# A two-block transformer pass on one Trainium2 core: norm sums in pieces, modulation vectors in the heads, and the state space's discretisation moved to the first output product

## The chip, the cores and the metric

The kernel runs on one core of one Trainium2 chip. The metric is the device time of one execution in microseconds (us); lower is better. In texts and rows PE is TensorE (PEld its weight loads), DVE is VectorE, ACT is ScalarE, POOL is GpSimd, SP is the engine that only issues transfers; a "q" behind a name is the engine's queue of waits, semaphores and DMA issues.

## What is computed

256 tokens of width 2048 go through two blocks, all in float32. Cut to what matters here:

```python
mod = silu(c) @ w_ada + b_ada              # 6 vectors of 2048: shifts, scales, gates
h = rmsnorm(x, g_mix) * (1 + sc1) + sh1
x = x + ga1 * (concat(rmsnorm(attn(h), g_attn), rmsnorm(lru(h), g_lru)) @ w_out)
h = rmsnorm(x, g_ffn) * (1 + sc2) + sh2
x = rmsnorm(x + ga2 * peer(h), g_final)    # peer: top-k experts
# second block, with its own c: s5 state space, then sparse attention
h = modulate(rmsnorm(x, g_l0), ...)
a, bb = s5_discretize(lam, log_step, b)    # exp, sin, cos, a quotient; no token enters
x = x + gate * s5_mixer(h, a, bb, ...)
x = x + gate * nsa_mixer(modulate(rmsnorm(x, g_l1), ...), kv(modulate(rmsnorm(x, g_kv), ...)))
return rmsnorm(x, g_final2)
```

rmsnorm divides by the root of the mean square over the 2048 channels. Channels lie on partitions, in 16 tiles of 128, so x is a buffer of 128 x 16 x 256.

## The kernel before

Each engine has its own hand-written program (`sync`, `tensor`, `scalar`, `vector`, `gpsimd`), and they meet only by semaphores. At a stage's end all four computing engines pass `meet` (L339), which waits for all of them.

**The stream.** All weights come as tiles of 1 MB through a ring of four slots (`load`, L384). SP issues them in one fixed order; a load waits until the slot's user of four loads ago has released it, and every later load waits behind it. `STAGES` (L52) gives each stage's tiles per round. A tile of a product is one 128-column output tile for TensorE (`gemm`, L465); a tile of a modulation matrix is a product with the vector silu(c) that VectorE makes in two halves with a running sum (`whole_vec`, `vec_sum`, L1383 to 1397).

**The first stage** has 8 rounds of four tiles: two for VectorE (the shift vector, `shift_part`) and two for TensorE (the scale vector, rows of one partition, L577). x is the fifth load. ScalarE issues the parameters and 19 transfers for the discretisation (many of them broadcasts of small tables over 16 or 64 partitions), then works on the discretisation between the stage's steps; GpSimd makes its elementwise part (L2021 to 2046) and VectorE the rest, between its tiles (L1474 to 1506). The result is written to memory (L1012) and read back before the recurrence.

**A norm** is a chain over four engines: ScalarE squares x into `SQ` in four calls (`norm_squares`, L954), TensorE multiplies ones with all 16 tiles (`norm_sums`, L548, float32 products run as two passes, so 32 instructions), VectorE takes mean and epsilon for 512 columns (`norm_rstd`, L1417; with one group both halves hold the same), ScalarE the root, VectorE the reciprocal of 512 columns, then 16 multiplications (`norm_scale`), which ScalarE follows with the shift (`norm_bias`). Each chain begins after a `meet`, but for the first, whose sums TensorE makes after its sixth tile. There are seven: mix, merged (two groups: attention and recurrence), ffn, final, l0 (its x is the result of final), l1, final2.

**The heads** are eight rounds of eight tiles: five products and three modulation vectors (positions 2, 5, 7). TensorE's order in a round is three products, the recurrence's gates, half a product, the scores, two halves, the transposes of probabilities, half a product, the attention (L600 to 640). VectorE makes the convolution, the vector of position 2, then waits for the scores and takes the row maxima; ScalarE needs these for the exponentials, VectorE scales the result, and TensorE transposes it.

**The first output product** (`w_out`) has 16 product tiles and 24 modulation tiles, in the order product, vector, product, vector, vector. VectorE adds each product to x when it is done (`residual`) and releases the bank; there are four banks. Its last vectors are shifts and scales of the ffn norm and the last gate. At the start of the next stage GpSimd multiplies the first two vector tiles of that stage (`vec_times`, L2051).

**Final and l0.** After the experts TensorE turns y back tile by tile (L731), VectorE adds it to x (L1789). Then all meet; norm final rewrites x, norm l0 follows in full, then all meet again and the recurrence starts with `fraction` on VectorE and the first product on TensorE.

**The end.** After the last product and a meeting, norm final2; when all 16 tiles are scaled, one transfer of 2 MB writes the result.

## Time and profile before

| what | value |
|---|---|
| runs shown | 3823.6, 3832.76, 3842.07 us (median 3832.76) |
| the profiled execution | 3838.9 us, span of its trace 3837.2 us, granted TensorE clock 0.962 of full |
| busy | PE 94%, PEld 82%, DVE 63%, ACT 35%, POOL 10% |
| instructions | 57514 |
| DMA | 817.73 MB, mean 213 GB/s |

The busy shares of 40 slices of 96 us, in tenths, and the granted clock of TensorE beside them:

```profile
PE   5799987999989999999999997999999899999997
DVE  5443454887547777777777776888816541655664
POOL 3000000420000000000000000677700000000000
PEclk9899999999999999999999998999999996999999
```

A low digit of PE is a stretch in which the engine that carries nearly all the work waits. The first slice is the first stage; the other dips lie at the norms. A clock below 1 in a row is a mean over stretches at the full 2.4 GHz and at 1.2 GHz.

### The profile page before, as it was taken

What the parts mean: (1) busy time and instruction counts of PE and PEld (TensorE: products, weight loads), DVE (VectorE), ACT (ScalarE), POOL (GpSimd) and SP (SyncE); (2) the same over time, 40 slices, a digit from 0 to 9 for tenths busy, and PEclk for the clock granted to TensorE, in tenths of its full rate; (3) what the DMA queues carried; (4) which work ended last, traced back from release to release, by engine and by line L of the source; (5) the groups of instructions that cost most, each with busy time, mean ns of one, the idle gap of its engine ahead of it and who ended that gap; (6) DMA issues with size and microseconds to landing.
All of it is one profiled execution on the core that took longest, in us unless ns stands there. A gap on an engine that the chain in (4) does not pass through costs nothing. (4 is left out here: it accounts for less than half of the span.)

```text
span 3837.2 us, 57514 instructions
## 1 busy us (share of the span) xinstructions
PE 3595.6 (94%) x21190; PEld 3148.6 (82%) x21190; DVE 2425.1 (63%) x4274; ACT 1333.5 (35%) x1967; POOL 390.2 (10%) x402
## 2 busy tenths in 40 slices
PE   5799987999989999999999997999999899999997
PEld 1488876778977999999999995666689899999997
DVE  5443454887547777777777776888816541655664
ACT  1233301212234444444444443211113442555553
POOL 3000000420000000000000000677700000000000
PEclk9899999999999999999999998999999996999999
DMA  8566666655665787887888774222247550555543
GB/s 322 196 226 210 221 241 250 227 203 168 234 258 210 285 297 290 301 300 285 298 288 297 289 290 154 77 87 87 88 154 252 213 179 22 180 182 188 186 170 116
DMA packets 123555, 817.73 MB, mean 213 GB/s; under 512 B 13345, under 2 KB 18721, under 8 KB 27169
## 3 DMA queue, kind: packets, MB, share of 16 engines
q1 hardware_dynamic: 105120, 760.26, 55.0%
q10 hardware_dynamic: 18304, 55.64, 3.8%
q8 instruction: 93, 1.52, 0.2%
q14 instruction: 38, 0.30, 0.0%
HBM read 791.66 MB, written 24.18 MB: 213 GB/s over the span
## 5 line engine op out<-in xcount | busy, mean ns | idle before, releaser
L473 PE MATMUL bank<-H,ring 128*128 128x256 f32 x4352 | 981.5, 384 | 44.8 <-ACT H L969 14.4
L473 PEld LDWEIGHTS bank<-H,ring 128*128 128x128 f32 x4352 | 826.5, 192 | 186.9 <-issue 68.5
L1683 DVE TENSOR_TENSOR vlo<-ring,vhi 128x1024 fp32r<-128x1024 f32 x448 | 548.2, 1225 | 312.1 <-ACT vhi L1141 295.5
L1141 ACT ACTIVATE vhi<-ring 128x1024 fp32r<-128x1024 f32 x448 | 475.0, 1061 | 632.8 <-PE bank L543 350.3
L1402 DVE TENSOR_TENSOR wlo<-ring,whi 128x1024 fp32r<-128x1024 f32 x240 | 293.8, 1225 | 324.0 <-ACT whi L946 317.4
L509 PE MATMUL bank<-Hhi,whi 128*128 128x256 f32 x1920 | 482.0, 288 | 16.4 <-DVE Hlo L1413 9.3
L510 PE MATMUL bank<-Hlo,whi 128*128 128x256 f32 x1920 | 475.3, 285 | 0.0
L536 PE MATMUL bank<-vhi,Ghi 128*128 128x512 f32 x1024 | 400.3, 391 | 0.0
L537 PE MATMUL bank<-vhi,Glo 128*128 128x512 f32 x1024 | 399.9, 391 | 0.0
L509 PEld LDWEIGHTS bank<-Hhi,whi 128*128 128x128 f32 x1920 | 370.0, 193 | 22.0 <-issue 16.2
L488 PE MATMUL bank<-Fhi,vhi 128*128 128x256 f32 x1536 | 374.4, 283 | 0.0
L489 PE MATMUL bank<-Flo,vhi 128*128 128x256 f32 x1536 | 373.6, 280 | 0.0
L510 PEld LDWEIGHTS bank<-Hlo,whi 128*128 128x128 f32 x1920 | 370.6, 193 | 0.0
L946 ACT ACTIVATE whi<-ring 128x1024 fp32r<-128x1024 f32 x240 | 253.9, 1059 | 313.1 <-PE bank L514 292.5
L489 PEld LDWEIGHTS bank<-Flo,vhi 128*128 128x128 f32 x1536 | 288.8, 188 | 0.5
L488 PEld LDWEIGHTS bank<-Fhi,vhi 128*128 128x128 f32 x1536 | 288.5, 188 | 0.5
L543 PE MATMUL bank<-vlo,Ghi 128*128 128x512 f32 x1024 | 276.4, 392 | 12.5 <-DVE vlo L1683 12.5
L1388 DVE CUSTOM_DVE_ANT_0 ring<-ring,cond 128x1024 f32<-128x1024 f32 x192 | 234.5, 1258 | 79.5 <-DMA ring<-in_w_ada 58.8
L514 PE MATMUL bank<-Hhi,wlo 128*128 128x256 f32 x1920 | 270.8, 284 | 0.0
L514 PEld LDWEIGHTS bank<-Hhi,wlo 128*128 128x128 f32 x1920 | 248.9, 192 | 0.0
L543 PEld LDWEIGHTS bank<-vlo,Ghi 128*128 128x128 f32 x1024 | 192.1, 188 | 56.0 <-DVE vlo L1683 15.8
L1760 DVE CUSTOM_DVE_ANT_0 arena<-arena,cond 128x1024 f32<-128x1024 f32 x192 | 233.8, 1218 | 0.0
(384 smaller groups left out, 4401.1 us busy)
## 6 DMA issues: line engine op xcount, KB each, us to landing
ring<-in_peer_u SPq DMA_DIRECT2D x128, 1024.0 KB, 5.0
ring<-in_peer_v SPq DMA_DIRECT2D x128, 1024.0 KB, 4.9
arena<-in_w_mod SPq DMA_DIRECT2D x96, 1024.0 KB, 6.7
ring<-in_w_ada SPq DMA_DIRECT2D x80, 1024.0 KB, 4.9
ring<-in_w_qz SPq DMA_DIRECT2D x64, 1024.0 KB, 4.8
ring<-in_w_in SPq DMA_DIRECT2D x40, 1024.0 KB, 4.8
ring<-in_w_mod SPq DMA_DIRECT2D x32, 1024.0 KB, 5.4
ring<-in_ssm_in SPq DMA_DIRECT2D x32, 1024.0 KB, 4.9
```

The source lines that it names most:

```text
L473: last = mm(out, ring[:, pos % R, k, :], rhs[:, k, :], start=(k == 0), stop=(k == KT - 1))
L488: mm(out, u_hi[:, k, :], Fhi[:, kk, :], start=(kk == 0), stop=False)
L489: mm(out, u_hi[:, k, :], Flo[:, kk, :], start=False, stop=False)
L509: mm(out, whi[:, half, k, :], Hhi[:, kk, :], start=(kk == 0), stop=False)
L510: mm(out, whi[:, half, k, :], Hlo[:, kk, :], start=False, stop=False)
L514: last = mm(out, wlo[:, half, k, :], Hhi[:, kk, :], start=False, stop=(kk == KT - 1))
L536: mm(pair[th][:], G_hi[part][:, n, tok], vhi[:, half, k, :], start=(n == 0), stop=False)
L537: mm(pair[th][:], G_lo[part][:, n, tok], vhi[:, half, k, :], start=False, stop=False)
L543: last = mm(pair[th][:], G_hi[part][:, n, tok], vlo[:, half, k, :], start=False, stop=(n == 7))
L1141: A(vhi[:, half], v_half(pos, half), ACT.Copy).then_inc(s("vhi_ready"), 1)
L1402: v.tensor_tensor(wlo[:, half], ring[:, pos % R, 8 * half:8 * half + 8, :], whi[:, half].bitcast(F32), ALU.subtract).then_inc(s("wlo_ready ...
L1683: v.tensor_tensor(vlo[:, half], v_half(pos, half), vhi[:, half].bitcast(F32), ALU.subtract)\
```

## The change

Four things are done together.

- **First stage.** The discretisation leaves it. Its inputs come as one prepared array in one transfer (`disc_in`), after the merged norm's scaling, and its instructions stand in the first output product: ScalarE's and GpSimd's as one block, VectorE's behind the additions of tiles 5 and 8 to 12. x is loaded after the fourth round, the sums of norm mix come after TensorE's 13th tile. The vector with c in columns is loaded first and passed on at once.
- **Heads.** Each head also loads three modulation vectors beside the ring, into a buffer of their own (`head_vec`), and VectorE multiplies them behind position 2. The first output product's stream is left with its 16 product tiles.
- **Norms in pieces.** ScalarE squares x in pieces of 4, 4, 4, 3 and 1 tiles, each as soon as VectorE has added the tiles (`new_squares` waits for the banks' releases); TensorE makes the sums directly behind the stage's last product, before the meeting. In the heads ScalarE squares each finished tile. Rows and reciprocals take one group only where there is one. Norm final and l0 share one pass: ScalarE also squares x times g_final, both sums are made, l0 is scaled from the unscaled x, and x itself is scaled later, in front of the recurrence.
- **The end.** The result leaves in four transfers, as its tiles are ready.

The diff, cut to its core and without the common indentation of a hunk:

```diff
-STAGES = dict(shift_scale=(4, 8, 4, 2), heads=(8, HEADS, 5, 3), w_out=(20, 2, 8, 12), topk=(20, 2, 12, 0),
+STAGES = dict(shift_scale=(4, 8, 4, 2), heads=(8, HEADS, 5, 3), w_out=(8, 2, 8, 0), topk=(20, 2, 12, 0),
...
+PIECES = ((0, 4), (4, 8), (8, 12), (12, 15), (15, 16))
+SQUARES = dict(mix=0, merged=5, ffn=21, final=26, l1=31, final2=36)
...
+def tile_done(stage, m):
+    before = list(BANK_USES)[:list(BANK_USES).index(stage)]
+    return 1 + sum(BANK_USES[b][m % 4 // 2] for b in before) + m // 4 + 1
...
-sp.dma_start(x[:], a["x"]).then_inc(x_loaded, 16)
-with sp.Fori(1, 8) as i:
-    for pos in range(4):
-        load("shift_scale", i, pos, a["w_scale" if pos % 2 else "w_ada"][2 * i + pos // 2])
+for lo, hi in ((1, 4), (4, 8)):
+    with sp.Fori(lo, hi) as i:
+        for pos in range(4):
+            load("shift_scale", i, pos, a["w_scale" if pos % 2 else "w_ada"][2 * i + pos // 2])
+    if lo == 1:
+        sp.dma_start(x[:], a["x"]).then_inc(x_loaded, 16)
...
+    if pos in (2, 4, 6):
+        n = pos // 2 - 1
+        sp.wait_ge(head_free[n], i + 1)
+        sp.dma_start(head_vec[:, n], a["w_ada"][56 + 3 * i + n].rearrange("p k n -> p (k n)"))\
+            .then_inc(head_loaded[n], 16)
-for m in range(4):
-    for k, pos in enumerate((0, 1, 2, 3, 4)):
-        src = a["w_out"][8 * i + 2 * m + k // 2] if k in (0, 2) else \
-            a["w_ada"][56 + 12 * i + 3 * m + (0, 0, 0, 1, 2)[k]]
-        load("w_out", i, 5 * m + pos, src)
+for pos in range(8):
+    load("w_out", i, pos, a["w_out"][8 * i + pos])
...
-sp.wait_ge(s("out_ready"), 1)
-sp.dma_start(a["out"], SQ).then_inc(s("stored"), 16)
-sp.wait_ge(s("stored"), 16)
+for j in range(4):
+    sp.wait_ge(s("out_ready"), 4 * j + 4)
+    sp.dma_start(a["out"][:, 4 * j:4 * j + 4, :], SQ[:, 4 * j:4 * j + 4, :]).then_inc(s("stored"), 16)
+sp.wait_ge(s("stored"), 64)
...
+def norm_sums(name):
+    for p, (lo, hi) in enumerate(PIECES):
+        pe.wait_ge(s("squares_ready"), SQUARES[name] + p + 1)
+        for t in range(lo, hi):
+            last = mm(WA[:, 0:T], ones[:, 0:P], SQ[:, t, :], start=(t == 0), stop=(t == KT - 1))
+    last.then_inc(s("sums_ready"), 1)
+def merged_sums():
+    for h in range(HEADS):
+        for g in range(2):
+            pe.wait_ge(s("squares_ready"), SQUARES["merged"] + 2 * h + g + 1)
+            last = mm((WA, WB)[g][:, 0:T], ones[:, 0:P], SQ[:, HEADS * g + h, :], start=(h == 0), stop=(h == HEADS - 1))
+    last.then_inc(s("sums_ready"), 1)
+def final_sums():
+    for p, (lo, hi) in enumerate(PIECES):
+        pe.wait_ge(s("squares_ready"), SQUARES["final"] + p + 1)
+        for t in range(lo, hi):
+            last = mm(WA[:, 0:T], ones[:, 0:P], SQ[:, t, :], start=(t == 0), stop=(t == KT - 1))
+        if hi == KT:
+            last.then_inc(s("sums_ready"), 1)
+        for t in range(lo, hi):
+            pe.wait_ge(s("scaled_squares"), t + 1)
+            last = mm(WB[:, 0:T], ones[:, 0:P], SQ2[:, t, :], start=(t == 0), stop=(t == KT - 1))
...
-    if kt == 5:
+    if kt == 12:
+pe.wait_ge(s("attn_ready"), HEADS + 1)
+merged_sums()
-norm_sums("merged", 2)
-        gemm("w_out", i, 5 * (g // 2) + 2 * (g % 2), banks[g % 4][:, 0:T], g % 4, uses[g % 4] + 2 * i + g // 4)
+        gemm("w_out", i, g, banks[g % 4][:, 0:T], g % 4, uses[g % 4] + 2 * i + g // 4)
+norm_sums("ffn")
-norm_sums("ffn")
...
-meet(pe, met)
-norm_sums("final")
-norm_sums("l0")
+final_sums()
+norm_sums("l1")
-norm_sums("l1")
+norm_sums("final2")
-norm_sums("final2")
...
-def norm_squares(name, src):
-    n = NORMS[name]
-    act.wait_ge(s("norm_src"), n + 1)
-    for j in range(4):
-        A(SQ[:, 4 * j:4 * j + 4, :], src[:, 4 * j:4 * j + 4, :], ACT.Square).then_inc(s("squares_ready"), 1)
+def squares(p, src):
+    lo, hi = PIECES[p]
+    A(SQ[:, lo:hi, :], src[:, lo:hi, :], ACT.Square).then_inc(s("squares_ready"), 1)
+def new_squares(stage, p):
+    for m in range(*PIECES[p]):
+        act.wait_ge(bank_free[m % 4], tile_done(stage, m))
+    squares(p, x)
-    A(sd[:], var[:], ACT.Sqrt).then_inc(s("sd_ready"), 1)
+    groups = slice(0, 2) if name == "merged" else slice(1, 2) if name == "l0" else slice(0, 1)
+    A(sd[:, groups], var[:, groups], ACT.Sqrt).then_inc(s("sd_ready"), 1)
...
+act.dma_start(vec[:], a["vec"]).then_inc(vec_in, 16)
-for name, dst in (("vec", vec[:]), ("w_f", w_f), ("b_f", b_f[:])):
+for name, dst in (("w_f", w_f), ("b_f", b_f[:])):
...
-act.dma_start(br_, a["ssm_b"]).then_inc(s("ssm_loaded"), 16)
+act.wait_ge(vec_in, 16)
+A(V("c_col"), V("c_col"), ACT.Silu).then_inc(s("c_col_ready"), 1)
-act.wait_ge(params, 48)
-A(V("c_col"), V("c_col"), ACT.Silu).then_inc(s("c_col_ready"), 1)
-act.sem_inc(s("norm_src"), 1)
-act.wait_ge(s("ssm_loaded"), 19 * 16)
...
-norm_squares("mix", x)
+for p in range(5):
+    squares(p, x)
-act.wait_ge(s("disc_b"), 1)
...
-act.wait_ge(s("disc_saved"), 16)
+act.wait_ge(params, 32)
...
+    act.drain()
+    A(SQ[:, bass.ds(i, 1), :], M[:, bass.ds(i, 1), :], ACT.Square).then_inc(s("squares_ready"), 1)
+    act.wait_ge(s("lru_done"), i + 2)
+    A(SQ[:, bass.ds(HEADS + i, 1), :], M[:, bass.ds(HEADS + i, 1), :], ACT.Square)\
+        .then_inc(s("squares_ready"), 1)
-act.sem_inc(s("norm_src"), 1)
-norm_squares("merged", M)
+act.wait_ge(s("merged_scaled"), 1)
+act.dma_start(disc_in, a["disc_in"]).then_inc(s("ssm_loaded"), 16)
+act.wait_ge(s("ssm_loaded"), 16)
...
+act.wait_ge(s("disc_b"), 1)
...
+act.wait_ge(s("disc_done"), 1)
+act.dma_start(a["disc"], disc).then_inc(s("disc_saved"), 16)
+for p in range(5):
+    new_squares("w_out", p)
+act.wait_ge(s("disc_saved"), 16)
-act.sem_inc(s("norm_src"), 1)
-norm_squares("ffn", x)
...
-meet(act, met)
-act.dma_start(disc, a["disc"]).then_inc(s("disc_loaded"), 16)
-act.dma_start(CC, a["ssm_c"]).then_inc(s("disc_loaded"), 16)
-act.sem_inc(s("norm_src"), 1)
-norm_squares("final", x)
+for p, (lo, hi) in enumerate(PIECES):
+    new_squares("turn", p)
+    if p == 0:
+        act.dma_start(disc, a["disc"]).then_inc(s("disc_loaded"), 16)
+        act.dma_start(CC, a["ssm_c"]).then_inc(s("disc_loaded"), 16)
+    for k in range(lo, hi):
+        A(SQ2[:, k, :], x[:, k, :], ACT.Square, scale=V("g_final")[:, k:k + 1]).then_inc(s("scaled_squares"), 1)
-norm_squares("l0", x)
...
+    if g in (5, 9, 13):
+        new_squares("ssm_out", g // 4 - 1)
+new_squares("ssm_out", 3)
+new_squares("ssm_out", 4)
-act.sem_inc(s("norm_src"), 1)
-norm_squares("l1", x)
...
-    v.tensor_scalar(var[:, 0:groups], WA[:, 0:groups * T].rearrange("p (a b) -> p a b", b=T),
-                    1.0 / width, EPS, ALU.mult, ALU.add)
-    if groups == 1:
-        v.tensor_scalar(var[:, 1], WA[:, 0:T], 1.0 / width, EPS, ALU.mult, ALU.add)
+    for g in range(groups):
+        v.tensor_scalar(var[:, g], (WA, WB)[g][:, 0:T], 1.0 / width, EPS, ALU.mult, ALU.add)
-    v.reciprocal(rstd[:], sd[:])
+    v.reciprocal(rstd[:, 0:groups], sd[:, 0:groups])
-def norm_scale(dst, src, g, signal=None):
+def norm_scale(dst, src, g, signal=None, groups=1):
-        ins = v.scalar_tensor_tensor(dst[:, k, :], src[:, k, :], g[:, k:k + 1], rstd[:, k // 8, :],
+        ins = v.scalar_tensor_tensor(dst[:, k, :], src[:, k, :], g[:, k:k + 1], rstd[:, k * groups // KT, :],
...
-shift_part(0, 3)
+shift_part(0, 7)
-shift_part(3, 4)
-lr, li = bl[:, 0], bl[:, 1]
-dve.wait_ge(s("disc_e"), 1)
-v.reciprocal(e[4], e[4])
...
+for n in range(3):
+    dve.sem_inc(head_free[n], 1)
+    for n in range(3):
+        dve.wait_ge(head_loaded[n], 16 * (i + 1))
+        for half in range(2):
+            w = head_vec[:, n, D // 2 * half:D // 2 * half + D // 2]
+            ins = v.tensor_tensor_reduce(w, w, cond[:, D // 2 * half:D // 2 * half + D // 2], 1.0, 0.0,
+                                         ALU.mult, ALU.add, accum_out=head_sums[:, half, n:n + 1])
+        ins.then_inc(head_free[n], 1)
+    dve.drain()
+    v.tensor_copy(mod_ab[:, :, bass.ds(56 + 3 * i, 3)], head_sums[:])
...
-norm_scale(H, M, V("g_merge"))
+norm_scale(H, M, V("g_merge"), groups=2)
-with dve.Fori(0, 2) as i:
-    for g in range(8):
-        m = g // 2
-        if g > 0:
-            residual("w_out", i, g - 1, 5 * ((g - 1) // 2) + 2 * ((g - 1) % 2), mod[:, 32:48])
-        if g % 2 == 0:
-            whole_vec("w_out", i, 5 * m + 1, 56 + 12 * i + 3 * m)
-        else:
-            whole_vec("w_out", i, 5 * m + 3, 57 + 12 * i + 3 * m)
-            whole_vec("w_out", i, 5 * m + 4, 58 + 12 * i + 3 * m)
-    residual("w_out", i, 7, 17, mod[:, 32:48])
+lr, li = bl[:, 0], bl[:, 1]
+for g in range(16):
+    residual("w_out", g // 8, g % 8, g % 8, mod[:, 32:48])
+    if g == 5:
+        dve.wait_ge(s("disc_e"), 1)
+        v.reciprocal(e[4], e[4])
+    if g == 8:
+        dve.wait_ge(s("disc_c"), 1)
+        tt(e[2], e[0], e[2], ALU.mult)
+        tt(e[3], e[0], e[3], ALU.mult)
+        dve.drain()
...
+    if g == 12:
+        tt(BB[:, 0], BB[:, 0], e[1], ALU.subtract)
+        tt(BB[:, 1], BB[:, 1], e[2], ALU.add)
+        dve.drain().then_inc(s("disc_done"), 1)
...
-meet(dve, met)
-norm_rstd("final", D)
-norm_scale(x, x, V("g_final"))
-dve.drain().then_inc(s("norm_src"), 1)
-norm_rstd("l0", D)
+v.tensor_tensor(gain[:, 2, :], gain[:, 2, :], V("g_final"), ALU.mult)
+dve.wait_ge(s("sums_ready"), NORMS["final"] + 1)
+v.tensor_scalar(var[:, 0], WA[:, 0:T], 1.0 / D, EPS, ALU.mult, ALU.add)
+dve.drain().then_inc(s("var_ready"), 1)
+v.reciprocal(var[:, 1], var[:, 0])
+dve.drain()
+dve.wait_ge(s("sums_ready"), NORMS["l0"] + 1)
+v.tensor_tensor(var[:, 1], WB[:, 0:T], var[:, 1], ALU.mult)
+dve.drain()
+v.tensor_scalar(var[:, 1], var[:, 1], 1.0 / D, EPS, ALU.mult, ALU.add)
+dve.drain().then_inc(s("var_ready"), 1)
+dve.wait_ge(s("sd_ready"), NORMS["l0"] + 1)
+v.tensor_tensor(rstd[:, 1], sd[:, 0], sd[:, 1], ALU.mult)
+dve.drain()
+v.reciprocal(rstd[:, 0], rstd[:, 1])
+dve.drain()
+v.tensor_tensor(rstd1, sd[:, 1], rstd[:, 0], ALU.mult)
...
+for k in range(KT):
+    v.scalar_tensor_tensor(x[:, k, :], x[:, k, :], V("g_final")[:, k:k + 1], rstd1, ALU.mult, ALU.mult)
-norm_scale(SQ, x, V("g_final2"))
-dve.drain().then_inc(s("out_ready"), 1)
+norm_scale(SQ, x, V("g_final2"), "out_ready")
...
+meet(pool, met)
+meet(pool, met)
-meet(pool, met)
-meet(pool, met)
-meet(pool, met)
```

## Rows read from the trace of the kernel before

**Rows 1.** The span cut into stretches: us, busy us of PE, PEld, DVE, ACT, POOL (instructions), PEclk, DMA share, GB/s
```profile
0.00:137.70 137.70, 79.08 (x192) 21.70 (x192) 80.46 (x108) 20.13 (x23) 31.92 (x41) 0.88 0.81 309
156.70:472.20 315.50, 315.46 (x1513) 273.24 (x1512) 128.35 (x278) 101.74 (x172) 0.00 (x0) 1.00 0.60 209
472.20:498.60 26.40, 10.08 (x32) 8.10 (x32) 13.73 (x27) 6.19 (x7) 0.00 (x0) 0.70 0.23 79
498.60:620.70 122.10, 115.84 (x512) 97.74 (x512) 68.15 (x135) 0.00 (x0) 0.00 (x0) 0.98 0.82 318
620.70:646.10 25.40, 8.74 (x33) 7.15 (x33) 13.82 (x24) 11.50 (x22) 9.44 (x4) 0.74 0.42 166
2354.00:2400.00 46.00, 18.91 (x64) 15.24 (x64) 22.33 (x44) 16.74 (x27) 0.00 (x0) 0.71 0.13 47
2998.00:3018.00 20.00, 8.75 (x32) 7.17 (x32) 7.86 (x13) 7.70 (x8) 0.00 (x0) 0.85 0.84 341
3808.30:3837.20 28.90, 8.83 (x32) 7.14 (x32) 11.02 (x20) 5.81 (x6) 0.00 (x0) 0.72 0.17 73
```

**Rows 2.** VectorE's groups in the first stage (busy us, mean ns), and from 460 to 640
```profile
L1388 DVE CUSTOM_DVE_ANT_0 ring<-ring,cond 128x1024 f32<-128x1024 f32 x32 | 45.1, 1447 | 36.3 <-DMA ring<-in_w_ada 20.0 <-ACT cond L990 15.5 <-issue 0.9
L1471 DVE TENSOR_TENSOR arena<-arena 128x1024 f32<-128x1024 f32 x16 | 18.7, 1220 | 0.3
...
L1388 DVE CUSTOM_DVE_ANT_0 ring<-ring,cond 128x1024 f32<-128x1024 f32 x52 | 61.6, 1222 | 39.6 <-DMA ring<-in_w_ada 38.8 <-issue 0.6
```

**Rows 3.** What SP's queue waited for, first stage: us in total, times, longest
```profile
SPq L387 <- DVEq L1391: 84.6, 14, 15.6
```

**Rows 4.** DMA of the first 140 us: GB/s in 40 slices, issues with us to landing; last line: the whole span's
```profile
GB/s 124 428 423 425 439 370 219 242 246 382 424 419 262 396 419 272 375 421 140 2 37 377 428 358 267 417 421 96 70 419 440 269 319 309 426 428 335 300 0 56
ring<-in_w_scale SPq DMA_DIRECT2D x16, 1024.0 KB, 7.8
arena<-in_ssm_b ACTq DMA_DIRECT2D x1, 1024.0 KB, 26.6
arena<-in_gate_w SPq DMA_DIRECT2D x1, 128.0 KB, 2.0
...
ring<-in_w_in SPq DMA_DIRECT2D x40, 1024.0 KB, 4.8
```

**Rows 5.** TensorE in order of time, first stage: start, us
```profile
57.23 7.17 PE L555 MATMUL work_a<-arena,ones 128*128 128x256 f32 x32
122.53 9.60 PE L577 MATMUL bank<-ring,vec 128*1 128x512 f32 x16 [6.90 <-DMA ring<-in_w_scale]
```

**Rows 6.** Seventh and eighth head in order of time: VectorE, then SP's queue
```profile
460.57 0.29 DVE L1554 TENSOR_REDUCE arena<-work_a 128x1 f32<-128x128 f32 x1 [14.69 <-PE work_a L621]
...
447.28 0.33 SPq L387 DMA_DIRECT2D ring<-in_w_in  x1
```

**Rows 7.** What TensorE waited for in the first output product: total, times, longest
```profile
PE bank L473 <- DMA ring<-in_w_out: 5.2, 9, 1.1
```

**Rows 8.** VectorE beside GpSimd in the first stage, and GpSimd behind the output product
```profile
52.17 2.01 DVE L1392 COPY mod_ab<-sums 128x2 f32 x1 [0.21 <-issue]
...
629.86 9.44 POOL L2056 TENSOR_TENSOR ring<-ring,cond 128x1024 f32<-128x1024 f32 x4 [561.01 <-DMA ring<-in_w_ada]
```

**Rows 9.** Around the final norm: the turning, ScalarE's one-tile activation (group), VectorE before the recurrence
```profile
2347.55 5.77 PE L731 MATMUL bank<-ident,y 128*128 128x128 f32 x32 [1.43 <-DVEq L1786]
...
L969 ACT ACTIVATE H<-arena,mod_ab 128x256 f32<-128x256 f32 x16 | 6.5, 494 | 4.0 <-DVE arena L1432 4.0
...
2411.34 0.70 DVE L1826 TENSOR_TENSOR work_d<-work_a,y 128x512 f32<-128x512 f32 x1 [6.36 <-PE work_b L757]
```

**Rows 10.** The norms' reciprocal and table load (ns min/median/max), and the last normalisation
```profile
L1427 DVE RECIPROCAL rstd<-sd x7: 3352/3353/3353, 65.9 to 3820.6; 128x512 f32<-128x512 f32 x7
...
L963 ACT ACT_TABLE_LOAD  x5: 1283/1283/1283, 43.9 to 3812.9; - x5
...
3824.01 6.42 DVE L1432 SCALAR_TENSOR_TENSOR arena<-x,vec,rstd 128x256 f32<-128x256 f32 x16
```

124 lines of the change are left out of this document (57 added, 67 removed).

## Prediction

> **What bounds the kernel now.** I read the cut into stages first [rows 1]. TensorE is busy 94% of the span, and inside the product stages it leaves nearly nothing: 315.46 of 315.5 us in the heads. An edit that only unloads another engine is worth nothing there. The time to be had is where TensorE stands still between products: the first stage (137.7 us, 79 busy), the four gaps around the norms (26.4, 25.4, 46.0 and 20.0 us), the tail (28.9 us), and some crumbs in the first output product. The change works on just these, so I price stage by stage.
>
> **First stage, 137.7 us.** Its real work is a stream of 32 weight tiles through four ring slots. SP stood waiting for VectorE's release of a slot for 84.6 us [rows 3], and VectorE spent 18.7 us on the discretisation's sixteen tensor operations [rows 2] and on a reciprocal of 1024 columns (twice the 3.35 us of 512 [rows 10], so 6.7), and was slowed meanwhile by GpSimd: the 32 vector products average 1447 ns, against 1222 ns where GpSimd is idle [rows 2]. The change takes all of it away, 25 us on VectorE and some 7 us of slowing, and with it small broadcast loads on ScalarE's queue; the first multiplications waited for them (their last big one took 26.6 us to land [rows 4]). What is left is bandwidth: 32 tiles and 3.4 MB of x, condition and parameters are 37 MB, 87 us at the 428 GB/s of the best slices [rows 4]. Around it lie about 3 us of start, the last tile's product (3.6 us) and the 5.5 us from TensorE's last product, 132.1, to the stage's end [rows 5, 1]: a floor of 99 us. My estimate is built from a ring round: a slot's transfer lands in 4.8 us mostly alone, 7.8 with neighbours [rows 4], the product takes 2.6 to 3.6, four tiles need 9.8 us of bandwidth; I take 10.5 us a round. VectorE and TensorE start at about 14 (condition, parameters and four tiles are 5.6 MB, 13 us at 428 GB/s). 14 + 8 x 10.5 + 5 (x, now behind round 4) + 2.5 (the norm's 32 sums, 7.17 us on TensorE [rows 5], now after tile 12 and mostly behind loads) + 5.5 = 111. **Saved: 27 us**; bounds 12 (no faster than the VectorE work removed allows, the rest lost to cold products, see the 9.60 us for two tiles in [rows 5] against 7.2 warm) and 38 (the floor).
>
> **Heads, 315.5 us.** Added per head on VectorE: three vectors of 2048, six products of 1.15 to 1.22 us, 7.2 us. They stand between the first vector and the row maxima, where VectorE idles 14.69 us until TensorE's scores [rows 6]. On SP: three more 1 MB loads per head, each with a wait in front, and the ring loads stand behind these waits; the releases they wait for come a whole head earlier, so they pass. The critical one is the third: SP reaches it behind the ring load of 447.28 [rows 6], it lands 5 to 7.8 us later at about 456, is multiplied by 458.3, and the scores come at 460.6. The DMA rate rises from 209 [rows 1] to about 290 GB/s, under the 428. On ScalarE two squares of 0.4 us at a head's end, where it idles long. **Price 0**; if the load is late the cover is 2.3 us plus about 2.5 us behind it; bound 16 us (2 a head).
>
> **Merged norm, 26.4 us.** Fourteen of 16 squares are ready when the last head ends (472.2). The old sums took 10.08 us, at a granted clock of 0.70 over the gap [rows 1], and began 4.6 us after the heads' end, behind the first squares; now the sums start at 473.3 and take 7.2: 480.5 against 486.9. The meeting now comes after them, and the two additions of the shift vectors after it, +1.0. **Saved 5.4.**
>
> **First output product, 122.1 us.** Only 16 of 40 tiles stay. TensorE's waits for tiles, 5.2 us [rows 7], go; the ramp of 2 us at its start stays. VectorE gets the discretisation, 26 us, between 16 additions; a product takes 7.1 us, so it has 114 us for 34, and four banks give 21 us of lee. GpSimd needs 29 us for its part, ScalarE 8: the last result is wanted by the ninth tile, 66 us in, and is there at about 47. **Saved 5.2**, bounds 0 and 7.
>
> **FFN norm, 25.4 us.** The squares run inside the product, the sums follow the last product directly: 7.2 us instead of 3.2 of squares and 8.7 of sums [rows 1], -4.7. The reciprocal takes half the columns, 1.7 instead of 3.35 us [rows 10], and one of two variance rows (0.35) and part of the root go: together -2.1. The vector additions and the gain (1.5 us) are now after the meeting, +1.5. That is -5.3. Against it: GpSimd's four products for the next stage, 9.44 us [rows 8], wait for nothing but the meeting now, since their tiles are long in the ring, and fall on just these small VectorE instructions. The trace shows one small copy, else 0.17 us, taking 2.01 beside GpSimd [rows 8], while the variance and the reciprocal in the same company ran at full speed. Four instructions of the chain can be held so, 2.3 us each at worst, the first normalisation again (it was held 2.1 us before, too). I take +4.3. **Saved 1**, bounds -3 and +6.
> The Trainium skill says which are held (GPSIMD Engine Reference, Specifications): the SBUF interface is shared, and it is VectorE instructions with two SBUF inputs or in a two-port mode that collide. By it all four small ones are exposed and the saving is 1; without the rule it would be 5.3. The row of the copy agrees.
>
> **Final norm and the first of the second block, 46.0 us.** Two chained norms become one: from the squares of x and of x times gain, both sums are made, 64 instructions, 14.3 us at full clock. TensorE turns until 2353.3 [rows 9], so the sums end at 2367.7; ScalarE is ahead (16 more squares, 0.4 to 0.49 us each [rows 9], done by 2361.5). Then about 6.5 us of small VectorE and ScalarE steps (two reciprocals of 1.7, one root between): the normalisation starts at 2374.2, before at 2393.1 (the 6.4 us of scaling and a meeting before the 2400 of [rows 1]). **Saved 18.9**, bounds 13 and 21. The scaling of x, 16 x 0.4 = 6.4 us, moves in front of the recurrence, where VectorE idles 6.36 us [rows 9]: +0.3; uncovered it would be 6.4.
>
> **Norm before the keys, 20.0 us.** Sums directly after the last product -5.6 (ScalarE's four DMA issues stood in front of the squares), narrower reciprocal -2.1, additions and gains after the meeting +1.8, the root's table, 1.28 us [rows 10], now behind the DMA issues +1.4: **saved 4.5**, bounds 2 and 6. **Tail, 28.9 us.** Sums -3.6, narrow reciprocal -2.1, meeting and table +1.2, and the result leaves in four parts. Scaling ended at 3830.4 [rows 10] and the span at 3837.2, 6.8 us for 2 MB; the last part is 512 KB, between the 2.0 us of a 128 KB load and the 4.8 of 1 MB (issue to landing) [rows 4]: 3.3. **Saved 8**, bounds 6 and 9.
>
> **Sum.** 27 + 0 + 5.4 + 5.2 + 1 + 18.9 - 0.3 + 4.5 + 8 = 69.7 us off the profiled execution's 3838.9 us (span 3837.2): 3769. That execution is 6 us above the median of the runs shown, 3832.8, so I predict 3763 to 3764 for the median.
>
> **Rivals.** *A, bandwidth already had most of the first stage*: it comes to 125 instead of 111, TensorE going cold between tiles; 3778. For: tiles in the clean end of the stage, without any discretisation, still came 5 to 8 us after issue. Against: SP's 84.6 us of waiting for VectorE. *B, everything near its good bound* (first stage 101, FFN chain not held): 3749. *C, the third vector is 2 us too late in each head*: 3780. *D, slower: that third load.* Issued at 448.1 and landing L us later, it delays the row maxima by L + 2.4 - 12.5 us; 2.3 us are covered, and each of eight heads pays the rest. The point of break-even with the 70 us is 8.7 us a head, L = 21. The trace has one load that took 26.6 us to land [rows 4], in the saturated first stage; so the heads lose 8 x 14.2 = 114 us, and the time is 3878. Against it: 209 GB/s in the heads, room for half as much again, and 5 to 8 us to landing even where SP issues four loads together. *E, the edits don't reach the path* (moved work surfaces in the output product, waits for the discretisation's saving holding the ffn squares): the norms in pieces bring nothing, 3764 + 5.4 + 1 + 18.9 + 4.5 = 3794, and if VectorE's 26 us surface in the output product as well, 3820.
>
> **How the numbers follow.** Forecast 0.50; A 0.17, B 0.12, C 0.12, D 0.03, E 0.06. The range takes in A, B and C and the sum's bounds as far as they are independent: 3738 to 3798. A measurement of this kernel can tell about 0.5%, 19 us, from no change. Faster by more: all but D and half of E, 0.94; same 0.03; slower 0.03.
>
> **What would show it.** First stage ending at 105 to 117, VectorE's products at 1.22 us throughout; the heads still 39.4 us apart (315.5 / 8) and no TensorE wait before its transposes; no wait for tiles in the output product; the gap before the query products still some 24 us, with held small instructions in it; 21 us between the last turning and the first state product's normalisation; a tail of 21 us. I am wrong if TensorE waits within a head, if the ring round is over 12 us, or if a norm's gap has grown.

## The result, and the profile after

The changed kernel takes 3744.4 us (median of four executions, 3742.9 to 3746.2) against 3831.0 us (3823.6 to 3842.1): a ratio of 0.977, 95% interval 0.975 to 0.980. The forecast was 3764, range 3738 to 3798. The sign and the size of the planned gains were right; a quarter of what the two profiles show came from stages that the forecast had put at nothing.

The profiled execution of the changed kernel has a span of 3744.5 us, 92.7 less than the one of before. The cut into the same stretches as [rows 1]; columns: us, busy us (instructions) of PE, PEld, DVE, ACT, POOL, PEclk, DMA share, GB/s.

```profile
0.00:114.90 114.90, 76.45 (x192) 20.22 (x192) 43.59 (x89) 11.44 (x14) 4.61 (x24) 0.91 0.85 341
133.90:449.40 315.50, 315.44 (x1513) 273.45 (x1512) 186.32 (x382) 106.83 (x186) 0.00 (x0) 1.00 0.76 292
449.40:471.00 21.60, 7.17 (x32) 6.00 (x32) 13.78 (x27) 3.02 (x5) 0.00 (x0) 0.74 0.29 98
471.00:585.20 114.20, 114.16 (x516) 100.11 (x517) 33.08 (x34) 11.07 (x13) 22.76 (x17) 0.97 0.48 167
585.20:609.10 23.90, 6.42 (x30) 5.32 (x28) 15.52 (x23) 8.95 (x20) 9.23 (x4) 0.73 0.25 88
2309.50:2336.30 26.80, 13.44 (x64) 11.53 (x62) 13.91 (x31) 15.08 (x34) 0.29 (x1) 0.83 0.11 45
2920.30:2937.00 16.70, 7.03 (x34) 5.88 (x33) 7.82 (x16) 5.31 (x8) 0.00 (x0) 0.82 0.84 334
3723.80:3744.50 20.70, 7.03 (x34) 5.85 (x32) 9.08 (x19) 2.12 (x3) 0.00 (x0) 0.73 0.25 102
```

In the second row 58 us more VectorE work and 83 GB/s more of transfers left the heads at 315.5 us to the tenth. In the fourth TensorE has no idle time left. To find what else moved, I cut both spans at the same instructions, to a few tenths of a us, and added everything up:

| stretch | before | after | saved | forecast |
|---|---|---|---|---|
| first stage | 137.7 | 114.9 | 22.8 | 27 |
| its normalisation, heads | 334.5 | 334.5 | 0 | 0 |
| merged norm | 26.4 | 21.6 | 4.8 | 5.4 |
| first output product | 122.1 | 114.2 | 7.9 | 5.2 |
| feed-forward norm | 25.4 | 23.9 | 1.5 | 1 |
| query stage, hot tokens | 443.9 | 442.7 | 1.2 | 0 |
| experts | 1257.5 | 1251.5 | 6.0 | 0 |
| turning to the recurrence's first product | 62.6 | 42.8 | 19.8 | 18.6 |
| **recurrence** | 376.6 | 363.4 | **13.2** | 0 |
| gating, output product | 211.3 | 210.8 | 0.5 | 0 |
| norm before the keys, up to the first key product | 21.7 | 16.7 | 5.0 | 4.5 |
| keys to the last product | 788.6 | 786.8 | 1.8 | 0 |
| tail | 28.9 | 20.7 | 8.2 | 8 |

One cut is looser: between the output product and the feed-forward norm the two rows before meet at the start of VectorE's last addition to x, the two after at its end. Cut at its start in both, the savings are 8.4 and 1.0; their sum stays.

The terms of the sum give 70.0 us of 69.7 forecast. The other 22.7 lie in stages that the forecast left alone and whose own work the change hardly touches, 13.2 of them in the recurrence. VectorE's group that makes a phase for the second half of a tile (busy us, mean ns), the kernel before:

```profile
L1804 DVE TENSOR_SCALAR var<-iota_t,arena 128x256 f32<-128x256 f32 x32 | 34.1, 1065 | 3.6 <-issue 3.3
```

The same group of the changed kernel:

```profile
L1865 DVE TENSOR_SCALAR var<-iota_t,arena 128x256 f32<-128x256 f32 x32 | 16.6, 519 | 3.5 <-issue 3.2
```

The same 32 instructions take half the time. What TensorE waited for behind the first tile's start (total, times, longest), before:

```profile
PE work_b L757 <- DVE arena L1835: 14.9, 15, 2.9
```

And changed:

```profile
PE work_b L795 <- DVE arena L1896: 3.5, 2, 2.9
```

Once in nearly every tile TensorE waited for VectorE; now it does so at the start, and for 0.6 us in the last tile. In order of time, one such spot of the kernel before: VectorE's phases, then GpSimd's product of the same moment.

```profile
2519.98 1.31 DVE L1804 TENSOR_SCALAR var<-iota_t,arena 128x256 f32<-128x256 f32 x1 [0.24 <-issue]
2521.21 0.47 DVE L1805 TENSOR_SCALAR work_d<-iota_t,arena 128x256 f32<-128x256 f32 x1
2521.60 0.96 DVE L1804 TENSOR_SCALAR var<-iota_t,arena 128x256 f32<-128x256 f32 x1
...
2519.87 1.27 POOL L2097 TENSOR_TENSOR arena<-arena,y 128x512 f32<-128x512 f32 x1 [0.67 <-DVEq L1837]
2521.09 1.31 POOL L2098 TENSOR_TENSOR arena<-arena,y 128x512 f32<-128x512 f32 x1
```

The same spot of the changed kernel:

```profile
2453.70 0.55 DVE L1865 TENSOR_SCALAR var<-iota_t,arena 128x256 f32<-128x256 f32 x1 [0.23 <-issue]
2454.56 0.42 DVE L1865 TENSOR_SCALAR var<-iota_t,arena 128x256 f32<-128x256 f32 x1
...
2448.96 0.76 POOL L2143 TENSOR_TENSOR arena<-arena,par 128x128 f32<-128x128 f32 x2 [3.13 <-PE work_c L806]
...
2453.38 0.72 POOL L2162 TENSOR_TENSOR arena<-arena 128x256 f32<-128x256 f32 x1 [0.21 <-issue]
2454.06 0.77 POOL L2163 TENSOR_TENSOR arena<-arena 128x256 f32<-128x256 f32 x1
2455.07 1.27 POOL L2158 TENSOR_TENSOR arena<-arena,y 128x512 f32<-128x512 f32 x1 [0.24 <-issue]
```

Here GpSimd had to wait 3.13 us for TensorE before its masks (L2143), so it is behind, and its products of 128 by 512 start only when the phases are done. It waits so in 14 tiles, 40.9 us in all; in the kernel before not once. A tile takes 22.75 us, TensorE's own time (it has no idle time from 2385 to 2680 us), instead of 23.46 and 23.9 in turns. These two patterns start from the same times: in the first tile, counted from TensorE's first small product, VectorE and GpSimd agree within 0.02 us in both kernels. TensorE does not. The stretch from 12 to 21 us after that product (columns as above), first of the kernel before:

```profile
2422.10:2431.10 9.00, 8.61 (x36) 5.80 (x37) 8.16 (x15) 1.59 (x3) 7.86 (x8) 1.00 0.01 3
```

The changed kernel:

```profile
2358.10:2367.10 9.00, 8.63 (x25) 5.52 (x25) 8.16 (x15) 1.62 (x3) 7.86 (x8) 0.64 0.01 3
```

Two of the experiments below, f_hold and then h_late, which both fell into the slower pattern:

```profile
2350.60:2359.60 9.00, 8.30 (x28) 5.82 (x28) 8.24 (x15) 1.30 (x3) 7.76 (x8) 0.81 0.01 3
```
```profile
2377.60:2386.60 9.00, 8.53 (x36) 5.73 (x37) 8.17 (x15) 1.50 (x3) 7.88 (x8) 1.00 0.01 3
```

In 9 us TensorE got through 36 instructions before and through 25 after, since its granted clock was 0.64 on average: at half for 9 x 0.36 / 0.5 = 6.5 us of the 9. So my theory, which was still to be tested, was odd: a slower clock in one tile puts TensorE 2.9 us behind, makes GpSimd's masks wait, and tips the loop of three engines into its faster pattern. The rivals: x scaled in front of the recurrence, or the new places of tiles and code.

### The profile page after: what moved, and what is told of

Same layout as the page of the kernel before. It is cut to its first block and busy times, and to the rows that moved or that the text cites. A ratio compares the mean times of both kernels' runs of the same rounds, so it can differ in the third digit from the quotient of the medians.

```text
span 3744.5 us, 57483 instructions
## 1 busy us (share of the span) xinstructions
PE 3569.6 (95%) x21190; PEld 3133.8 (84%) x21190; DVE 2386.0 (64%) x4257; ACT 1337.4 (36%) x1996; POOL 385.5 (10%) x402
## 5 line engine op out<-in xcount | busy, mean ns | idle before, releaser
L557 PEld LDWEIGHTS bank<-vhi,Ghi 128*128 128x128 f32 x1024 | 192.9, 188 | 41.4 <-issue 0.6
```

The costliest lines, as they stand in the source:

```text
L557: mm(pair[th][:], G_hi[part][:, n, tok], vhi[:, half, k, :], start=(n == 0), stop=False)
```

## Experiments

Ratios are to the kernel before; "recurrence" is from TensorE's first small product to its last one in the profile of the run.

**1. r_pe_late: the kernel before, TensorE late once.**
```diff
-                for ri in range(2):
+                for ri in list(range(2)) * times:
...
-                b_times_u(i, t, 3)
+                b_times_u(i, t, 3, times=4 if first else 1)
```


> The kernel before, with three repeats of one small product of the recurrence (same operands, same result) in its first tile, so that TensorE falls some 3.2 us behind once. Theory, phase: the recurrence's 376.4 us were a loop paced by VectorE, in which GpSimd's products fall on VectorE's phase instructions (1.31 and 0.96 us where 0.35 to 0.43 would do); TensorE 3 us late once makes GpSimd's mask step wait for TensorE, and the loop settles at 22.75 us a tile instead of 23.67, as in the changed kernel, where TensorE ran 2.9 us late in the first tile at half the clock. Then the recurrence takes 363 to 366 us, its phase instructions come down from 34 to about 17 us, and the whole is 10 us shorter than before (ratio 0.9975), although work was added. Rival, the gain comes from something else in the change (x scaled in front, other places of tiles and code): the recurrence takes 376 to 380 us and the whole is the same or 3 us longer.

Profile: recurrence 366.4 us, span 3824.2, 13.0 less than the profile of before. But the ten executions lay at 3824.9 to 3838.2, median 3829.2, and the thirteen of the kernel before, run beside them, at 3824.8 to 3838.7, median 3829.5: ratio 1.000 (0.999 to 1.001). The expected 10 us are not there as a mean. And the profiled execution had a dip of the clock of its own at the same spot (0.66 over 9 us), so it does not tell the repeats from the dip. There was also little to gain: ten of the thirteen executions of the kernel before lay at 3830.5 or below, so most of them were probably fast by themselves. So this run does not show that a late TensorE tips the loop. What it shows is that the fast pattern exists in the old kernel, with no line of the change in it: neither the scaling of x in front of the recurrence nor the new places of tiles and code are needed for it.

**2. r_bubble: the changed kernel, VectorE late once.**
```diff
             ssm_tile(0, 0, first=True)
+            for _ in range(4):
+                v.tensor_tensor(P1, P2, P2, ALU.mult)
+                dve.drain()
```


> The changed kernel, with four idle products on VectorE (about 3 us, their results are used by nothing) behind the recurrence's first tile. Theory, phase: TensorE, 2.9 us behind there, catches up, and the loop falls back into the pattern paced by VectorE, 23.67 us a tile: the recurrence takes 363.3 + 3 + 10 to 13 = 376 to 379 us, and the whole some 13 to 16 us more than the changed kernel: 3759 against 3744, a ratio to the kernel before near 0.981. Rival, TensorE is the bound and any 3 us of VectorE are absorbed or cost just themselves: 363 to 366 us, ratio 0.977 to 0.978.

Measured: 3765.0 us (3763.8 to 3766.8), ratio 0.983 (0.982 to 0.985), 20.6 more than the changed kernel. The bubble took 5.8 us where I had expected 3, so the whole is past the 13 to 16 us expected. This profile had the same dip of the clock (0.64) as the changed kernel, and yet fell into the slow pattern: a dip is not enough for the fast one. By the theory VectorE's delay let TensorE catch up. The phase instructions' groups (ns, min/median/max):

```profile
L1865 DVE TENSOR_SCALAR sd<-iota_t,arena x32: 353/968/1400, 2333.4 to 2685.7; 128x256 f32<-128x256 f32 x32
L1865 DVE TENSOR_SCALAR var<-iota_t,arena x32: 344/967/1320, 2336.0 to 2698.3; 128x256 f32<-128x256 f32 x32
```

The second group in the changed kernel:

```profile
L1865 DVE TENSOR_SCALAR var<-iota_t,arena x32: 344/428/1129, 2338.6 to 2682.1; 128x256 f32<-128x256 f32 x32
```

And the recurrence of r_bubble as one stretch:

```profile
2343.50:2726.30 382.80, 365.31 (x1504) 252.22 (x1504) 323.57 (x557) 70.50 (x123) 275.21 (x316) 0.97 0.23 85
```

The median of the second group is 967 ns, in the changed kernel 428. A bubble of 5.8 us cost 19.4 us in the recurrence: the theory's 5.8 and 13.

**3. f_hold: GpSimd's vector products wait for the norm.**
```diff
+            pool.wait_ge(s("scaled_ready"), 2 * KT)
             with pool.Fori(0, 2) as i:
```


> The changed kernel, with GpSimd's vector products for the query stage waiting until VectorE has normalised all of x for the feed-forward norm. Theory of the prediction: the three small VectorE instructions held at 2.2 us each (0.18 elsewhere) run at full speed, and the gap before the query products shrinks by 4.3 to 6.1 us, from 24.4 to between 18.3 and 20.1; the whole is 4 to 6 us shorter than the changed kernel, ratio near 0.976. Rival 1: the held instructions are short, but ScalarE's table load and root stand next in line, gain under 1 us. Rival 2: the products, 9.2 us later, release their ring slots 16 us later, and TensorE waits for tiles in the first query products: the gap shrinks, and up to 6 us come back as waits behind it.

The gap between the sums and the query products shrank by 6.1 us. In order of time, the changed kernel:

```profile
592.04 2.27 DVE L1494 TENSOR_TENSOR mod_ab<-mod_ab,vec 128x24 f32<-128x24 f32 x1
594.39 2.21 DVE L1484 TENSOR_SCALAR gain<-mod_ab 128x16 f32<-128x16 f32 x1
596.67 2.22 DVE L1486 TENSOR_TENSOR gain<-gain,vec 128x16 f32<-128x16 f32 x1
...
591.93 9.23 POOL L2118 TENSOR_TENSOR ring<-ring,cond 128x1024 f32<-128x1024 f32 x4 [87.11 <-PEq L364]
```

This one:

```profile
588.76 0.18 DVE L1494 TENSOR_TENSOR mod_ab<-mod_ab,vec 128x24 f32<-128x24 f32 x1
589.01 0.17 DVE L1484 TENSOR_SCALAR gain<-mod_ab 128x16 f32<-128x16 f32 x1
589.26 0.18 DVE L1486 TENSOR_TENSOR gain<-gain,vec 128x16 f32<-128x16 f32 x1
```

Three held instructions, at the 2.2 to 2.3 us that the prediction named as the worst for each. By the start of the experts 2.7 of the 6.1 us are gone again. Where, among TensorE's waits in the query stage of this kernel:

```profile
PE work_a L708 <- DVE arena L1667: 19.9, 4, 8.7
```

These waits for VectorE's selection were 14.9 us in the changed kernel. Rival 2 saw the give-back and had the wrong waiting place (tiles). The four executions lie at 3739.8, 3740.2, 3751.2 and 3751.7 (ratio 0.978, 0.975 to 0.980): two groups 11 us apart. So the median, 3745.7, is not the 4 to 6 us shorter that I expected; the lower group alone is, by 4. The profiled one is of the upper group, and its recurrence took 375.6 us: the clock was at half for 9 x 0.19 / 0.5 = 3.4 us only, and TensorE not late enough.

**4. s_slots: seven buffers instead of four in the first stage.**
```diff
+            for m in range(KT):
+                if m >= 3:
+                    sp.wait_ge(head_free[m % 3], m // 3)
+                sp.dma_start(head_vec[:, m % 3], a["w_ada"][m].rearrange("p k n -> p (k n)")).then_inc(head_loaded[m % 3], 16)
+                load("shift_scale", m // 4, m % 4, a["w_scale"][m], first=m < 4)
...
```


> The changed kernel, with the first stage's vector tiles loaded into the three head vector buffers and only the scale tiles into the four ring slots: seven buffers instead of four, same bytes, same products. Theory: the ring round of 12 us is set by the handshake (SP waited 55.5 us for TensorE's releases and 30.8 for VectorE's), not by bandwidth (353 GB/s over most slices, 426 at best); with seven buffers the stream runs near 426 GB/s, and the stage ends at 101 to 106 instead of 115.2 us: 9 to 14 us off, ratio near 0.974. Rival: what the DMA engines deliver in this pattern of loads is already the limit, or TensorE's cold products are; the stage ends at 112 to 116.

In this and the later experiments the first stage's end is the start of VectorE's normalisation, 0.3 us behind the cut of the tables (115.2 for 114.9, 138.0 for 137.7). The stage ended at 105.7 us. The changed kernel's code for it ended at 115.2, 110.9, 111.9, 112.6, 112.9 and 111.7 us in the six profiles that have it (mean 112.5), so seven buffers are worth some 7 us, less than the 9 to 14 expected from the one profile at 115.2. The stretch from 30 to 50 us, changed kernel:

```profile
30.00:50.00 20.00, 13.90 (x29) 2.24 (x26) 9.21 (x20) 0.00 (x0) 0.00 (x0) 0.91 0.91 356
```

This one:

```profile
30.00:50.00 20.00, 14.50 (x33) 2.35 (x32) 10.19 (x20) 0.00 (x0) 0.00 (x0) 1.00 1.02 428
```

428 GB/s is the rate of the best slices of [rows 4]: in this stretch the bandwidth is now the bound. Four executions at 3733.8, 3733.8, 3740.2, 3751.0; ratio 0.977 (0.974 to 0.979).

**5 and 6. r_fix and r_fix_bubble: the slow pattern taken away.**
```diff
                     pool.wait_ge(s("z_ready"), 4 * tile + j + 1)
+                    if j == 2 and not last:
+                        pool.wait_ge(s("frac_ready"), 2 * tile + 4)
```


> The changed kernel, with GpSimd's products of a tile's third pair held until VectorE has made the phase of the next tile's second half. The run with the bubble took 382.8 us in the recurrence and the run with TensorE late 366.5, so there are two patterns, and an execution falls into one of them. Theory: the cost in the slow one is GpSimd's 128 by 512 products beside VectorE's phase instructions (1.31 and 0.96 us instead of 0.35 and 0.43, 1.5 us a tile); kept apart, VectorE needs 22.2 us a tile, less than TensorE's 22.75, and only the fast pattern is left: the recurrence takes 363 to 366 us in the profile, and the single executions lie within 4 us of one another, near 3744. Rival: GpSimd, 1.9 us later in each tile, becomes the bound; 370 to 380 us.

> The kernel with GpSimd held as just described, and the idle VectorE products behind the first tile as well (they took 5.8 us, not 3). Theory: with the collision gone the loop has no slow pattern to fall into, and the bubble costs itself or less: the recurrence takes 363 to 370 us where the same bubble made it 382.8, and the whole is at most 6 us over the kernel without it, 3744 to 3751. Rival, the slow pattern comes from something else than the held phase instructions: 378 to 384 us again, 3760 and more.

r_fix: 3745.0 us (3741.0 to 3746.2), ratio 0.976 (0.974 to 0.978), recurrence 361.7 us in an execution whose clock did not dip (1.00 over the 9 us), so TensorE was not late. r_fix_bubble: 3749.2 us (3746.5 to 3752.4), ratio 0.977 (0.975 to 0.980), recurrence 367.9 us. The same bubble costs 6.2 us instead of 19.4. Phases of r_fix:

```profile
L1865 DVE TENSOR_SCALAR sd<-iota_t,arena x32: 352/806/1419, 2336.6 to 2668.2; 128x256 f32<-128x256 f32 x32
L1865 DVE TENSOR_SCALAR var<-iota_t,arena x32: 337/350/724, 2339.3 to 2680.5; 128x256 f32<-128x256 f32 x32
```

The phases of the second half (var) are no longer held (median 350 ns). Those of the first half (sd) are not: inside the recurrence they average 905 ns in r_fix, 698 in the changed kernel. So the wait moves part of the collision to where it costs the loop nothing.

**7. b_fix: the same two lines in the kernel before.**

> The kernel before, with GpSimd's products of each tile's third pair held until VectorE has made its phases, and nothing else. In the changed kernel this made the recurrence 361.7 us and the executions 3741 to 3746. Theory: the two patterns of the recurrence are also what spreads the executions of the kernel before over 3823 to 3843 us; with one pattern left the recurrence takes 361 to 366 us instead of 376.4, and the executions lie within 5 us at 3822 to 3828, a ratio near 0.997 to 0.998; then the change itself is worth 3825 less 3745, some 80 us. Rival: the spread comes from elsewhere, and the executions still lie over 15 us.

Ten executions at 3819.9 to 3825.3, median 3822.7. Of the nineteen of the kernel before beside them, twelve lie at 3821.2 to 3827.9 and seven at 3835.8 to 3842.4, with nothing between. Only the profiled executions show their recurrence, so that the two groups are the two patterns is a conclusion: their medians are 16 us apart, the recurrences of the profiles 13 to 15 (376.6 us before, 363.4 in the changed kernel, 361.6 in b_fix), and b_fix has only the lower group. The ratio, 0.999 (0.998 to 1.000), is small because most executions of before drew the fast pattern in this batch. With the draw taken out of both, the change is worth 3822.7 - 3745.0 = 77.7 us. The table without the recurrence gives 79.5: 70.0 of the change's own terms, 6.0 of the experts and 3.5 of crumbs.

**8. v_work: VectorE's work back in the first stage.**
```diff
...
+            shift_part(0, 4)
+            v.reciprocal(f[:, 7], g0)
...
+            for n in (2, 4, 2):
+                extra(n)
```


> The changed kernel, with sixteen products and a reciprocal of 1024 columns given back to VectorE in the first stage, in batches between its vector products (their results are used by nothing; GpSimd and the parameter loads stay out of the stage). The first stage ended at 110.9 to 115.2 us in three executions of this code. Theory 1, VectorE's own work was what the stage paid for, all of it: the stage ends at 136 to 141. Theory 2, in each 12 us round VectorE is idle for some 5 us and absorbs that much of a batch of 9.4: the stage ends at 121 to 127, and the rest of what the change gained there (138 to 111) was GpSimd's slowing of the vector products and the small loads. The whole 3754 to 3771 accordingly.

`extra(n)` makes n products of 128 by 1024; with the rest of the edit there are sixteen, and the reciprocal. VectorE was busy for 68.7 us of the stage instead of 43.6, and the stage ended at 117.7, 5 us after the mean of 112.5 (2.5 to 6.8 after the single ones). That is below both theories: even the batches of 9.4 us were nearly covered. The whole took 3760.0 us (3748.9 to 3764.1), ratio 0.979 (0.977 to 0.982), with the slow pattern in the profile (recurrence 375.1), which is more of it than the stage.

**9. b_loads: one dense load instead of nineteen, in the kernel before (with b_fix's lines).**
```diff
...
-            for k in range(8):
-                act.dma_start(bl[16 * k:16 * k + 16], a["lam_tile"][k:k + 1].broadcast_to([16, 2, KT, 64]))\
-                    .then_inc(s("ssm_loaded"), 16)
...
+            act.dma_start(disc_in, a["disc_in"]).then_inc(s("ssm_loaded"), 16)
```


> The kernel before with the same hold on GpSimd, and in the first stage one load of 2.1 MB, laid out beforehand, in place of the nineteen small and broadcast loads of the discretisation's inputs. The 25 us of VectorE work given back to the changed kernel cost its first stage only some 5 us (117.7 against 110.9 to 115.2), so most of the 23 to 27 us gained there must be in something else. Theory: in the kernel before the DMA engines were full at 22 to 32 us while they moved only 180 to 320 GB/s, and VectorE waited 9.5 and 5.6 us for tiles there; with one dense load the stage ends at 128 to 133 instead of 138. Rival 1: the loads moved as many bytes as now and cost nothing: 136 to 139. Rival 2: GpSimd starts the discretisation earlier, so that it slows vector products all the same and the gain is given back: 134 to 137.

The stage ended at 130.7 us, against 137.0 in b_fix and 138.0 before: 6 to 7 us. The stretch from 22 to 32 us of the kernel before:

```profile
22.00:32.00 10.00, 5.33 (x13) 0.93 (x11) 0.41 (x2) 0.00 (x0) 0.00 (x0) 1.00 1.02 237
```

And of this one:

```profile
22.00:32.00 10.00, 7.14 (x14) 1.14 (x13) 2.85 (x3) 4.22 (x6) 3.94 (x2) 0.98 1.00 416
```

The engines are full in both; the small loads let them move 237 instead of 416 GB/s. The whole: 3820.9 us, 1.8 under b_fix, ratio 0.998 (0.996 to 0.999). In the two profiles the lead of 6.3 us is kept and reaches the recurrence as 7.4. There 3.1 of it go: the clock was at 0.62 over the 9 us of the first tile, in b_fix at 1.00. Another 1.7 go behind it; why stays open.

**10. h_late: the third vector of each head 6 us later.**
```diff
-                    if pos in (2, 4, 6):
+                    if pos in (2, 4, 7):
```


> The changed kernel, with each head's third vector loaded behind the head's last ring load instead of in front of it, about 6 us later. In the last head its product ended 0.7 us before the scores came. Theory of the prediction (a cover of some 2 us in front of the row maxima and 2.5 behind): the row maxima come some 5 us late, TensorE waits 2 to 3 us in each of eight heads, the heads take 332 to 340 us instead of 315, and the whole 3760 to 3770. Rival, the cover behind the row maxima is larger than I took, or the load lands as early as before since SP's waits overlap: the heads take 315 to 320 us, the whole 3744 to 3749.

The heads took 336.9 us instead of 315.5, 2.7 each. They as one stretch:

```profile
129.90:466.80 336.90, 325.30 (x1513) 278.10 (x1512) 185.35 (x382) 106.91 (x186) 0.00 (x0) 0.97 0.71 271
```

What TensorE waited for in it:

```profile
PE work_b L672 <- DVEq L1595: 8.0, 8, 1.7
PE bank L667 <- ACTq L1072: 3.6, 3, 1.2
```

TensorE waits 11.6 us, and is busy for 9.8 more: its granted clock is 0.97 on average, where it was 1.00. The whole took 3770.3 us (3757.8 to 3779.3), ratio 0.982 (0.979 to 0.985). The profiled execution is the slowest of the four, with the slow pattern on top of the heads; the spread of 21 us I have not explained. So the mechanism of rivals C and D is real and stood 6 us away; the change has the load just early enough.

**11 and 12. best and best2: what the experiments pay for, together.** Both have r_fix, s_slots and, at the norms, this:
```diff
-            pe.wait_ge(s("merged_scaled"), 1)
...
+                        if made:
+                            pe.wait_ge(s(made[0]), made[1] + k + 1)
```


> The changed kernel with four edits: seven buffers in the first stage, GpSimd held in the recurrence, GpSimd's vector products held until the feed-forward norm's small steps are done (and no longer), and TensorE starting on each quarter stage as the norm delivers: the product behind each of four norms waits for one 128 by 256 piece at a time instead of for all sixteen. From the gaps of the changed kernel: the first piece is there some 0.9 us after VectorE's first scaling, the last 6.5 us later, and sixteen steps of a product take 6.9 us, so each of the four starts 6 us earlier and ends about 6 us earlier. The sum: 4 times 6, 7 from the first stage (105.7 against 112.7 on average), 6 from the held instructions, less 3 for waits behind the query products: 3745 less 34 is 3711, range 3703 to 3722, ratio to the kernel before 0.967 to 0.971. Rival: TensorE starts at half the clock, so that the steps spread over the norm's delivery are run slowly and two thirds of the four gains are given back: 3727.

Measured: 3720.1 us (3719.4 to 3723.2), ratio 0.973 (0.970 to 0.975), 9 short of the sum and nearer to the middle between it and the rival. The starts behind the first norm and the merged norm came 6.5 and 6.3 us earlier, with no loss behind them. Two places failed. GpSimd, released at the first piece, held the normalisation that I wanted to feed TensorE with, and before the recurrence nothing moved (13.3 us between the sums and the product, 13.4 before), since all engines still met behind the last piece. The first of the two in order of time, VectorE and GpSimd in best:

```profile
572.53 14.78 DVE L1476 SCALAR_TENSOR_TENSOR arena<-x,gain,rstd 128x256 f32<-128x256 f32 x16
...
573.35 10.12 POOL L2122 TENSOR_TENSOR ring<-ring,cond 128x1024 f32<-128x1024 f32 x4 [86.34 <-DVE arena L1476]
```

In every other run of the changed kernel's code these sixteen take 6.42 us. Before, where the first of them met GpSimd too, they took 8.51. best2 holds GpSimd to the last piece and moves the meeting in front of the normalisation.

> The kernel of the last run but for two places. GpSimd's vector products for the query stage wait until VectorE has normalised all sixteen pieces: released at the first piece, they held VectorE's normalisation at 14.8 us instead of 6.4, and TensorE stood between its pieces. And the meeting of the engines in front of the state space stands ahead of the normalisation instead of behind it: TensorE's wait for the pieces one by one gained nothing there (the gap stayed at 13.3 us), because the meeting waited for ScalarE's last piece all the same. Theory: the query product's first pieces follow at TensorE's own pace (8 us off, of which 3 to 5 come back as waits for VectorE behind the scores), the first state product starts 6 us earlier: 3720 less 9 to 11 is 3710, range 3705 to 3716. Rival: GpSimd's masks and the clock at half speed take the second gain back: 3715 to 3720.

Measured: **3714.3 us** (3711.7 to 3715.5), ratio 0.970 (0.967 to 0.972), 30 us under the changed kernel. The gap before the state product fell from 13.3 to 7.6 us; VectorE's scaling of x, formerly covered, now ends 2.6 us after the recurrence could start.

## Why the prediction was right, step by step

**First stage: right in its sum, wrong in its reason.** The forecast was an end at 111; six profiles of that code give 110.9 to 115.2, mean 112.5. I put the gain to VectorE's 25 us and GpSimd's slowing of 7. But given back alone, in the changed kernel, the work costs 5 us (v_work), and the small loads, which I only named, cost 6 to 7 in the kernel before (b_loads). SP's 84.6 us of waiting [rows 3] counted waits, many of which end in slack: VectorE itself was idle for 57 of the 137.7 us [rows 1], 20.0 of them waiting for tiles [rows 2]. The other 13 of the 25 us may lie in GpSimd's slowing and in the norm's chain and x, which stood in the middle of the stream; these I have not separated. The products did come down from 1447 to 1224 ns, as forecast. My ring round of 10.5 us was 12 in the profile, just at the bound that I had named as a sign of being wrong; the four slots' handshake holds it there, since with seven buffers it is 10. TensorE began at 9.5 us and not at my 14. So the sum holds in part by luck: 9.5 + 8 x 12 + 5 for x is 110.5, where TensorE's last product ends, against 105.5 in my sum.

**Heads: right**, and closer than I thought. I gave the third vector a cover of 2.3 us; in the last head its sum was ready 0.7 us before the scores.

**First output product: undersized.** It saved 7.9 (8.4 by the stricter cut), not 5.2: the tile waits, and some 2.5 us in the products themselves. A tile's product took 7.04 to 7.17 us before and 6.91 after, both at the full clock of 1.00; why, I have not followed. The ramp stayed, as I had said: the first product ended 9.7 us after its start before and 10.1 after. VectorE's discretisation was covered as counted: it still idled for 1.7 us or more before every addition but the one behind its reciprocal.

**Feed-forward norm: right for the reason given.** I took 4.3 us for held instructions, 6.2 were there (three of 2.2 us instead of 0.18), and the saving was 1.5 instead of 1 (1.0 by the stricter cut). I had named four small ones and the first normalisation: one of the four ran 0.16 us ahead of GpSimd, and the normalisation, behind it, took 6.42 us. The Trainium skill (GPSIMD Engine Reference, Specifications) has VectorE instructions with two SBUF inputs or in a two-port mode collide with GpSimd. Two of the three held ones agree (two inputs, 0.18 or 2.2 us), and so do the sixteen normalisations (6.42 us in all, 14.78 beside GpSimd in best). The third (L1484) and the phases of the recurrence have one tensor input and were held as well, 2.21 instead of 0.17 us and 1.31 instead of 0.35; whether they ran in that mode no run shows.

**Final norm, norm before the keys, merged norm, tail:** 19.8, 5.0, 4.8, 8.2 against 18.6, 4.5, 5.4, 8. These were counts of instructions by durations from rows of the same kernel, and here they held within 1.2 us.

**What the prediction missed** is that I took the recurrence for unchanged because its code is. Its loop of VectorE, GpSimd and TensorE has two patterns, 13 us apart, and by the grouped times each execution draws one. That GpSimd's products beside the phases make the slow one is shown by r_bubble and r_fix_bubble; what tips an execution into one or the other is not. The kernel before was profiled in the slow one, which I could have seen: one group of phase instructions at 1065 ns beside its sister at 476, and executions 18 us apart with nothing to explain it. The changed kernel seems to have drawn the fast one in all four executions: they lie at 3742.9 to 3746.2, those of r_fix, which has no other, at 3741.0 to 3746.2. So 87 us of difference in the medians contain some 9 of this.

## What to carry to other kernels

A loop in which three engines hand work round can have more than one steady pattern; if executions of a kernel fall into two groups, look for an instruction whose duration differs between them, and separate the two that collide by a wait: here one wait cost nothing and took 13 us of chance away. A queue's waiting time is no price: give the work back alone and measure, before calling it the cause. And a gap behind a norm is worth feeding piece by piece, but only if nothing slows the pieces and no meeting of the engines stands behind the last.
